# Token halves transposed behind the halves of the projection, and token roots of two orders read back from memory

## The chip, the cores and the metric

The program runs on one core of one Trainium2 chip. The metric is the device time of one execution in microseconds (us). A core has five engines with a queue each: TensorE (PE, with its weight loads as PEld), VectorE (DVE), ScalarE (ACT), GpSimd (POOL) and SyncE (SP), which here only issues transfers.

## The reference

Two groups of tokens, 512 and 1024 of them, go through two layers that share their weights. Each layer is a mixer and then a routed mixture of 16 experts:

```
for layer in range(DEPTH):
    h = rms_norm(x, norm_mix[layer])
    x = x + (mixer_ab if layer % 2 == 0 else mixer_c)(h, ...)
    h = rms_norm(x, norm_ffn[layer])
    x = x + expert_choice_moe(h, w_router[layer], w_gate[layer], w_up[layer], w_down[layer])
```

`rms_norm` multiplies a token by one over the root of its mean square (the token's root) and by a gain. `mixer_ab` projects h once and runs two kinds of attention: A, three patterns of local attention with keys at strides 1, 4 and 16 (a1, a4, a16), and B, dense attention over all keys. `mixer_c` is local attention with a sink. Queries and keys are normed per head and rotated before the scores. All of it is float32.

## The kernel before

The 1536 tokens are 12 tiles of 128. Attention runs in three phases of `attention_phase`: "b" and "a" in the first layer, "c" in the second, each followed or surrounded by output and expert phases that the change leaves alone. In a phase, a list `events` written by class `Work` sets the order of the work, and every engine walks the same list and does its share of each event. The events are:

- ("N", n, half): half of a raw token tile, 512 of its 1024 columns, is brought into hTh and hTl. PE transposes it in four pieces into a room of PSUM (`turn_x`, L971), ACT copies it out as the high part (`x_high_part`, L669), DVE subtracts to get the low part (`x_low_part`, L796). The half came into xb by a transfer that SP issues (`load_x`, L544).
- ("P", p, half): half of the projection of tile p, twelve matmuls (L151 to L153). After the second half ACT empties the result (`evacuate`, L680 and L681) and squares it for the head norms (L688).
- ("T", p): the normed queries and keys of p are transposed by PE (L995, L998), copied by ACT, split by DVE (the last step is kT, L839).
- ("S", u), ("R", u), ("V", g): scores, transposes of the probabilities (L1021) and the product with V (L1037). ("W", q): a quarter of the weights is split by ACT (L658) and DVE (L788).

Tile p is projected while the unit five tiles back is in R and V. In "b" the token tiles are transposed within the first ten projections, in "c" likewise. Phase "a" does six turns of 12 tiles, two for each pattern. Patterns a4 and a16 need the tokens in another order (`order` 1 and 2), so while the second turn of one pattern is projected, the tiles of the next are transposed anew into hTh and hTl. That makes 24 tiles, or 48 halves, in phase "a", beside 24 halves each in "b" and "c".

Every N, T and R takes the next room of psT, and there are two rooms, used in turn. The transpose that takes a room waits until the one two rooms earlier has been copied out (`room_free`). For an N room that is x_low, DVE's subtraction. In phase "a" one tile uses the rooms R (one, or two where the unit has six key blocks), T, N of half 0, N of half 1.

Token roots: after each N, ACT squares the half in place and sums it (`x_square`, L665). POOL turns two sums into the root rt and the term em (`token_root`, four instructions). `load_x` of a later half waits for the squaring (x_squared), because it writes the same buffer; there are 4, 2 and 3 buffers xb in "b", "a" and "c".

Of the kernel before, what the change touches and what calls it, by code (L numbers as in the profile page):

```python
# [7 lines left out]
F32 = mybir.dt.float32  # L8
# [7 lines left out]
P = 128  # L16
SEQ, DEC_SEQ = 512, 1024
TOK = SEQ + DEC_SEQ
NT = TOK // P
# [4 lines left out]
GROUPS = 4  # L24
# [9 lines left out]
WQ = 4  # L34
# [183 lines left out]
class Work:  # L218
# [41 lines left out]
    def projection(self, p, norm):  # L260

        got = []
        for half in range(2):
            if norm is not None and p:
                got.append(("N", norm, half))
            got.append(("P", p, half))
            if self.dense and p and p % NT == 0 and half == 0:
                got += [("W", p // NT * WQ + 2), ("W", p // NT * WQ + 3)]
        if norm is not None and not p:
            got += [("N", norm, 0), ("N", norm, 1)]  # L270
        return got
# [125 lines left out]

def attention_phase(nc, state, name, steps, hT, roots, x_rows, norm_gain, identity, masks, mask0, table, sink=None,
                    ring=None, loaded=None, split=False, follow=None, w_out=None):
# [10 lines left out]
    hTh, hTl = hT  # L410
    rt, em = roots
    NS = len(steps)
# [82 lines left out]
    half_ready, tally = ph.sem("half_ready"), ph.sem("tally")  # L495
    mask_in = ph.sem("mask_in")
    NCONST, NMASK = 1 + NS, (masks is not None) + (sink is not None)
# [17 lines left out]
    def raw_quarter(q):  # L515

        return raw[:, spot_of(q), :, 0:cols(q)]
# [12 lines left out]
    with nc.Block() as block:  # L530

        @block.sync
        def _(sp):
            halves = 2 * len(work.norms)

            def load_x(x):
                if x >= halves:
                    return
                i, t = work.norms[x // 2]
                if x >= XH:  # L540

                    sp.wait_ge(x_squared, x - XH + 1)
                rows = token_rows(x_rows, t, work.kinds[i])
                sp.dma_start(xb[:, x % XH], rows[:, x % 2 * HC:(x % 2 + 1) * HC]).then_inc(x_in[x % XH], 16)  # L544

            def load_w(q):
                if q >= own + WQ * (follow is not None):
                    return
                if q >= RING:

                    i, quarter = divmod(q - RING, WQ)
                    sp.wait_ge(projected, 2 * (i * NT + NT - 1) + quarter // 2 + 1)
                sp.dma_start(raw_quarter(q), weights(q)).then_inc(w_in[(q - have) % RING], 16)

            def load_constants():
# [30 lines left out]
            load_w(4)  # L586
            load_w(5)
            for e in events:
                if e[0] == "N" and 2 * e[1] + e[2] >= early:
# [14 lines left out]
        def _(pool):  # L604
# [36 lines left out]
            for e in events:  # L641
                if e[0] == "N" and e[2] == 1:
                    token_root(e[1])
                if e[0] == "P" and e[2] == 1:
                    if first:
                        pool.wait_ge(const_in, 16 * NCONST)
                        first = False
                    head_roots(e[1])

        @block.scalar  # L650
        def _(act):
# [20 lines left out]
            def evacuate(p):  # L672
                b, (s, _, t) = p % 2, place(p)
                if p >= 2:
                    act.wait_ge(gained, p - 1)
                n = [work.norm_of[i, t] for i in range(p // NT + 1) if (i, t) in work.norm_of]
                if n:
                    act.wait_ge(rt_ready, n[-1] + 1)
                act.wait_ge(projected, 2 * p + 2)
# [59 lines left out]
            for e in events:  # L739
                if e[0] == "N":  # L740
                    x_high_part(e[1], e[2])
                    to_square.append(e[1:])
                    if e[1] == 0 and not dense:
                        squares()
# [1035 lines left out]
def encoder(nc, a, stop=99):  # L1780
# [13 lines left out]
    with ExitStack() as ctx:  # L1794
# [3 lines left out]

        rt = ctx.enter_context(nc.sbuf_tensor("rt", [P, 3, NT], F32))
        em = ctx.enter_context(nc.sbuf_tensor("em", [P, 3, NT], F32))  # L1800
        roots = (rt, em)
        ident = ctx.enter_context(nc.sbuf_tensor("ident", [P, P], F32))
# [23 lines left out]
        with high(0) as wh:  # L1826
            with nc.sbuf_tensor("hTh", [P, KD, TOK], F32R) as hTh, nc.sbuf_tensor("hTl", [P, KD, TOK], F32R) as hTl:
                attention_phase(nc, state, "b",
                                [dict(kind="b", nq=B_NQ, nkv=1, order=0, w=a["w_b"], gain=a["gain_b"], out=by_tile(ob, B_NQ))],
                                (hTh, hTl), roots, x_rows, a["gain_mix"][0], a["identity"], None, 0, a["rope_axial"],  # L1830
                                ring=dict(kept, high=wh, first=0), follow=dict(w=a["w_a"][0][0], cols=6 * HD))
# [3 lines left out]
                                (hTh, hTl), roots, x_rows, a["gain_mix"][0], a["identity"], a["masks"][:, 3 * P:], 3 * P,  # L1835
                                a["rope_a"], ring=dict(kept, high=wh, first=GROUPS * WQ), loaded=arrivals["c_in"], split=True,
                                w_out=out_weights(a["w_out_ab"], "ab_out"))
# [3 lines left out]
        with high(1) as wh:  # L1841
            with nc.sbuf_tensor("hTh1", [P, KD, TOK], F32R) as hTh, nc.sbuf_tensor("hTl1", [P, KD, TOK], F32R) as hTl:
                attention_phase(nc, state, "c",
                                [dict(kind="c", nq=C_NQ, nkv=1, order=0, w=a["w_c"], gain=a["gain_c"], out=by_tile(oc, C_NQ))],
                                (hTh, hTl), roots, y_rows, a["gain_mix"][1], a["identity"], a["masks"][:, 0:3 * P], 0, a["rope_c"],
                                a["sink"], ring=dict(kept, high=wh, first=0), loaded=arrivals["c_in"],
                                w_out=out_weights(a["w_out_c"], "c_out"))
# [52 lines left out]
```

## Time and profile before

| | |
|---|---|
| time, median of 3 runs | 4019.5 us (4018.96 to 4022.48) |
| the profiled execution | 4020.69 us, span 4018.3 us |
| PE busy | 3811.2 us, 95% of the span |
| DVE, ACT, POOL busy | 67%, 53%, 22% |
| mean granted PE clock | 0.975 of full speed |

Times within the trace are in us from the start of the span. Phase "b" ends at 680, "a" runs from 682 to 1190, "c" from 2360 to 2851; the rest is output and expert phases.

### The profile page before, as it was taken

The numbers are of one execution on the slowest core, as the hardware profiler recorded it, in microseconds if no ns is written. First come the engines' busy times: TensorE is split into PE (matmuls) and PEld (weight loads), VectorE is DVE, ScalarE is ACT, GpSimd is POOL, SyncE is SP. The second block draws the span as 40 slices with busy tenths as digits, with TensorE's granted clock in tenths as the row PEclk, the third lists the DMA queues.
The fourth block names the chain that finished last, engine by engine and source line by source line (L and its number), as shares of the span: only waits on it lengthen the run. The fifth ranks groups of instructions, "written<-read, shape, count | busy, mean of one in ns | idle before, by whom it ended". The sixth has DMA issues, their size and how long they took to land. (4 is left out here: it accounts for less than half of the span.)

```text
span 4018.3 us, 75219 instructions
## 1 busy us (share of the span) xinstructions
PE 3811.2 (95%) x27032; PEld 3678.0 (92%) x27032; DVE 2677.1 (67%) x5533; ACT 2138.5 (53%) x3992; POOL 891.0 (22%) x1463
## 2 busy tenths in 40 slices
PE   7999999999979889999999979999896999999998
PEld 7989988999978689999999979999785999999998
DVE  6665664766665677777777747777536777777775
ACT  6554554666642255565556546555323565656554
POOL 5132220444430011111111133332000111211112
PEclk9999999999989889999999989999997999999999
DMA  3000001122124377887788721000335778777874
GB/s 106 11 22 7 25 16 35 46 67 68 52 95 150 128 244 246 250 251 241 245 250 251 242 83 47 32 22 16 136 137 189 238 250 255 244 240 249 255 244 131
DMA packets 489001, 583.91 MB, mean 145 GB/s; under 512 B 18512, under 2 KB 444496, under 8 KB 488784
## 3 DMA queue, kind: packets, MB, share of 16 engines
q1 hardware_dynamic: 470928, 522.40, 39.6%
q0 software_dynamic: 15680, 50.34, 5.8%
q10 hardware_dynamic: 2176, 8.39, 0.5%
q8 instruction: 122, 2.00, 0.2%
q14 instruction: 95, 0.78, 0.1%
HBM read 514.86 MB, written 66.21 MB: 145 GB/s over the span
## 5 line engine op out<-in xcount | busy, mean ns | idle before, releaser
L1654 DVE TENSOR_TENSOR wl<-raw,wh 128x2048 fp32r<-128x2048 f32 x384 | 879.2, 2290 | 284.9 <-ACT wh L1609 271.9
L1609 ACT CAST wh<-raw 128x2048 fp32r<-128x2048 f32 x384 | 733.1, 1909 | 24.2 <-DMA raw<-in_w_gate 21.9
L1753 PE MATMUL ps_g<-xT,wh 128*128 128x384 f32 x2048 | 599.1, 359 | 3.2 <-DVE xT L1660 3.2
L1753 PE MATMUL ps_u<-xT,wh 128*128 128x384 f32 x2048 | 594.8, 357 | 0.0
L1755 PE MATMUL ps_g<-xT,wl 128*128 128x192 f32 x2048 | 478.9, 254 | 0.0
L1755 PE MATMUL ps_u<-xT,wl 128*128 128x192 f32 x2048 | 477.1, 253 | 0.0
L151 PE MATMUL psP<-ring_high,hTh 128*128 128x384 f32 (+1 forms) x1344 | 464.4, 346 | 12.3 <-ACT V L681 5.1
L153 PE MATMUL psP<-ring_high,hTl 128*128 128x384 f32 (+1 forms) x1344 | 445.5, 331 | 0.0
L152 PE MATMUL psP<-ring_low,hTh 128*128 128x384 f32 (+1 forms) x1344 | 445.4, 331 | 0.0
L1037 PEld LDWEIGHTS psO<-V,pT 128*128 128x128 f32 x3456 | 419.8, 192 | 19.1 <-issue 11.7
L1037 PE MATMUL psO<-V,pT 128*128 128x64 f32 x3456 | 416.3, 273 | 3.7 <-ACT pT L725 3.6
L1755 PEld LDWEIGHTS ps_g<-xT,wl 128*128 128x128 f32 x2048 | 388.4, 191 | 0.0
L1755 PEld LDWEIGHTS ps_u<-xT,wl 128*128 128x128 f32 x2048 | 385.8, 190 | 0.0
L1753 PEld LDWEIGHTS ps_g<-xT,wh 128*128 128x128 f32 x2048 | 378.5, 190 | 3.5 <-issue 3.5
L1753 PEld LDWEIGHTS ps_u<-xT,wh 128*128 128x128 f32 x2048 | 376.1, 189 | 0.0
L713 ACT ACTIVATE prob<-psS,nbias 128x384 f32<-128x384 f32 (+4 forms) x480 | 308.1, 648 | 77.3 <-DVE nbias L860 41.1
L725 ACT COPY pT<-psT 128x512 f32<-128x512 f32 (+2 forms) x348 | 182.9, 540 | 242.8 <-PE psT L1021 237.8
L625 POOL TENSOR_TENSOR xg<-xr,gains 128x256 f32<-128x256 f32 (+1 forms) x168 | 130.2, 775 | 785.3 <-ACT V L681 747.5
L151 PEld LDWEIGHTS psP<-ring_high,hTh 128*128 128x128 f32 x1344 | 256.8, 191 | 17.9 <-ACT V L681 7.9
L1556 POOL COPY put_s<-idx 128x1 uint32 x30 | 5.5, 182 | 1185.7 <-DVE cp L1673 1185.7
L1021 PE MATMUL psT<-ident,prob 128*128 128x128 f32 x1728 | 245.1, 276 | 14.5 <-DVE pT L912 4.7
L805 DVE TENSOR_REDUCE ss<-xn 128x4 f32<-128x256 f32 (+1 forms) x168 | 73.6, 438 | 276.3 <-ACT xn L688 276.3
(204 smaller groups left out, 8901.6 us busy)
## 6 DMA issues: line engine op xcount, KB each, us to landing
raw<-in_w_gate SPq DMA_DIRECT2D x128, 1024.0 KB, 5.4
raw<-in_w_up SPq DMA_DIRECT2D x128, 1024.0 KB, 5.2
raw<-in_w_down SPq DMA_DIRECT2D x128, 1024.0 KB, 8.3
xb<-in_x SPq DMA_DIRECT2D x72, 256.0 KB, 2.8
out_y<-yb SPq DMA_DIRECT2D x24, 512.0 KB, 2.6
h_rows<-hb SPq DMA_DIRECT2D x24, 512.0 KB, 3.0
ring_raw<-in_w_a SPq DMA_DIRECT2D x24, 384.0 KB, 4.3
xb<-in_x SPq DMA_DIRECT2D x12, 512.0 KB, 4.9
```

Of the source, the lines that this page charges most:

```text
L151: eng.matmul(out, ah, bh, start=start, stop=False)
L152: eng.matmul(out, ah, bl, start=False, stop=False)
L153: return eng.matmul(out, al, bh, start=False, stop=stop)
L625: pool.tensor_tensor(xg[:, b, :], xr[:, b, :], gains[:, s, :], ALU.mult).then_inc(gained, 1)
L713: ins = act.activation(prob[:, u % 2, c * KC:c * KC + nk * P], psS[:, u % 2, c * 512:c * 512 + nk * P], ACT.Exp, bias=nbias[:, g % 4, x:x ...
L725: act.copy(pT[:, slot, at:at + w], room_of("R", u, k)[:, 0:w]).then_inc(pT_act, 1)
L1021: ins = pe.transpose(room_of("R", u, k)[:, x * P:(x + 1) * P], prob[:, u % 2, c * KC + j * P:c * KC + (j + 1) * P], ident)
L1037: ins = pe.matmul(psO[:, (off + c) * HD:(off + c + 1) * HD], pT[:, slot, at + x * P:at + (x + 1) * P], V[:, k0 + j, kv * HD:(kv + 1) * HD] ...
L1609: act.copy(wh[:, j % SPL], raw[:, j % RAW]).then_inc(w_high, 1)
L1654: dve.tensor_tensor(wl[:, j % SPL], raw[:, j % RAW], wh[:, j % SPL].bitcast(F32), ALU.subtract)\
L1753: both = lambda **fl: pe.matmul(ps[:, f, 0:2 * CAP], wh[:, j % SPL, k, fs], xT[:, k].rearrange("p h c -> p (h c)"), **fl)
L1755: high = lambda: pe.matmul(ps[:, f, 0:CAP], wl[:, j % SPL, k, fs], xT[:, k, 0, :], start=False, stop=False)
```

## The change

Two things are edited. First, `projection` puts each half of the projection ahead of the N of the same number; this concerns all three phases. Second, phase "a" no longer squares its token tiles. The roots of order 0, which phase "b" has computed, are stored to a small tensor in memory, one root and one term for each token, and read back in the orders of a4 and a16 by four transfers with pieces of 8 bytes. `rt` and `em` become the two columns of one tensor `roots`. In phase "a" `load_x` then waits for PE's transpose of the buffer (x_turned) in place of the squaring.

```diff
@@ projection @@
         for half in range(2):
+            got.append(("P", p, half))
             if norm is not None and p:
                 got.append(("N", norm, half))
-            got.append(("P", p, half))
@@ attention_phase @@
-    rt, em = roots
+    rt, em = roots[:, :, :, 0], roots[:, :, :, 1]
+    squaring = name != "a"
@@ load_x @@
                 if x >= XH:
-
-                    sp.wait_ge(x_squared, x - XH + 1)
+                    sp.wait_ge(x_squared if squaring else x_turned, x - XH + 1)
@@ sync @@
+            def reorder_roots():
+                sp.dma_start(roots_out.rearrange("(t p) x -> p t x", p=P), roots[:, 0]).then_inc(roots_stored, 16)
+                sp.wait_ge(roots_stored, 16)
+                for s, st in enumerate(steps[1:], 1):
+                    for first, n in ((0, SEQ), (SEQ, DEC_SEQ)):
+                        stride = STRIDES[st["kind"]][first > 0]
+                        rows = roots_out[first:first + n].rearrange("(u p r) x -> p r u x", p=P, r=stride)
+                        at = roots[:, s, first // P:(first + n) // P].rearrange("p (r u) x -> p r u x", r=stride)
+                        sp.dma_start(at, rows).then_inc(roots_in, 16)
...
             load_w(4)
             load_w(5)
+            if not squaring:
+                reorder_roots()
@@ gpsimd @@
-                if e[0] == "N" and e[2] == 1:
+                if squaring and e[0] == "N" and e[2] == 1:
                     token_root(e[1])
@@ evacuate @@
-                n = [work.norm_of[i, t] for i in range(p // NT + 1) if (i, t) in work.norm_of]
-                if n:
-                    act.wait_ge(rt_ready, n[-1] + 1)
+                if squaring:
+                    act.wait_ge(rt_ready, work.norm_of[0, t] + 1)
+                elif p % (NT * turns) == 0 and s:
+                    act.wait_ge(roots_in, 32 * s)
@@ scalar @@
                     x_high_part(e[1], e[2])
-                    to_square.append(e[1:])
+                    if squaring:
+                        to_square.append(e[1:])
```

Three places show what moves. The first is PE in phase "a", in the second turn of pattern a1, from the end of a projection to the scores of the next tile; the names in brackets are the semaphores waited on, x_low being the low part of an N. Before:

```order
L153 MATMUL psP<-ring_high,hTl 128x384
L1037 MATMUL psO<-V,pT 128x64 [waits pT_act_2,o_done_2]
L1037 MATMUL psO<-V,pT 128x64 x2
L1037 MATMUL psO<-V,pT 128x64 [waits pT_dve_2]
L1037 MATMUL psO<-V,pT 128x64 x2
L1021 MATMUL psT<-ident,prob 128x128 [waits x_low_2,exp_done_2]
L1021 MATMUL psT<-ident,prob 128x128 x2
L1021 MATMUL psT<-ident,prob 128x128 [waits x_low_2]
L1021 MATMUL psT<-ident,prob 128x128 x2
```

The same place with the change (14 lines were added above, so L971 is L985, L1037 is L1051 and L1021 is L1035):

```order
L153 MATMUL psP<-ring_high,hTl 128x384
L985 MATMUL psT<-ident,xb 128x128 [waits low_out_2,x_in1_2]
L985 MATMUL psT<-ident,xb 128x128 x3
L1051 MATMUL psO<-V,pT 128x64 [waits pT_act_2,o_done_2]
L1051 MATMUL psO<-V,pT 128x64 x2
L1051 MATMUL psO<-V,pT 128x64 [waits pT_dve_2]
L1051 MATMUL psO<-V,pT 128x64 x2
L1035 MATMUL psT<-ident,prob 128x128 [waits x_low_2,exp_done_2]
L1035 MATMUL psT<-ident,prob 128x128 x2
L1035 MATMUL psT<-ident,prob 128x128 [waits x_low_2]
L1035 MATMUL psT<-ident,prob 128x128 x2
```

The transposes of the second token half have come from ahead of the twelve matmuls to behind them; the second x_low that the R waits for belongs to that half.

The second place is ACT in phase "a", one tile from the exponentials to the copy of the next probabilities. Before:

```order
L713 ACTIVATE prob,den<-psS,nbias 128x256
L669 CAST hTh<-psT 128x4x128 [waits x_turned_2]
L665 ACTIVATE xb,ssx<-xb 128x512 [waits rt_ready_2]
L669 CAST hTh<-psT 128x4x128 [waits x_turned_2]
L665 ACTIVATE xb,ssx<-xb 128x512 [waits rt_ready_2]
L680 COPY xr<-psP 128x256 [waits projected_2,gained_2]
L681 ACTIVATE V<-psP,rt 128x128
L688 ACTIVATE xn<-xr 128x256 [waits turned_2,evacuated_2]
L725 COPY pT<-psT 128x512 [waits pv_done_2,p_turned_2]
```

The same tile with the change:

```order
L726 ACTIVATE prob,den<-psS,nbias 128x256
L681 CAST hTh<-psT 128x4x128 [waits x_turned_2]
L693 COPY xr<-psP 128x256 [waits projected_2,gained_2]
L694 ACTIVATE V<-psP,roots 128x128
L701 ACTIVATE xn<-xr 128x256 [waits turned_2,evacuated_2]
L681 CAST hTh<-psT 128x4x128 [waits x_turned_2]
L738 COPY pT<-psT 128x512 [waits pv_done_2,p_turned_2]
```

Both squarings are gone, and the cast of the second half now stands behind the three instructions that empty and square the projection.

The third place is SP at the start of phase "a", with the change:

```order
L553 DMA ring_raw<-in_w_a 128x768 x2
L556 DMA roots_out<-roots 128x12x2
L563 DMA roots<-roots_out 128x8
L563 DMA roots<-roots_out 128x8x2
L563 DMA roots<-roots_out 128x8
L563 DMA roots<-roots_out 128x16
L610 DMA arec<-osb 128x132 x6
```

Before, the first output stores (arec) follow directly on the two weight quarters (ring_raw); now the store and the four loads of the roots stand between them.

## Rows read from the trace of the kernel before

**Rows 1.** The page, busy time, its share of the span, instructions.

```profile
PE 3811.2 (95%) x27032; PEld 3678.0 (92%) x27032; DVE 2677.1 (67%) x5533; ACT 2138.5 (53%) x3992; POOL 891.0 (22%) x1463
```

**Rows 2.** Groups by line and shape, 756 to 1040: busy, mean ns | idle before, releasers.

```profile
L971 PE MATMUL psT<-ident,xb 128*128 128x128 f32 x192 | 29.9, 279 | 10.6 <-DVE kT L839 6.0 <-ACT pT L725 3.1 <-DVE pT L912 1.5
```

**Rows 3.** Timeline around a tile of phase "a": start, duration, engine, line, [idle before <-releaser].

```profile
804.07 1.00 PE L1037 MATMUL psO<-V,pT 128*128 128x64 f32 x8
804.32 0.37 ACT L680 COPY xr<-psP 128x256 f32<-128x256 f32 x1 [0.66 <-PE psP L153]
804.90 0.83 PE L1021 MATMUL psT<-ident,prob 128*128 128x128 f32 x6
804.99 0.42 ACT L688 ACTIVATE xn<-xr 128x256 f32<-128x256 f32 x1
...
808.60 0.63 PE L971 MATMUL psT<-ident,xb 128*128 128x128 f32 x4 [1.16 <-DVE pT L912]
...
808.99 0.42 PE L151 MATMUL psP<-ring_high,hTh 128*128 128x384 f32 x1
```

**Rows 4.** Timeline in the fill of phase "b", all engines.

```profile
43.69 0.59 ACT L669 CAST hTh<-psT 128x512 fp32r<-128x512 f32 x1 [0.84 <-PE psT L971]
...
44.31 0.69 DVE L796 TENSOR_TENSOR hTl<-psT,hTh 128x512 fp32r<-128x512 f32 x1 [0.90 <-ACT hTh L669]
...
46.10 0.28 DVE L827 TENSOR_SCALAR xn<-xg,rstd 128x128 f32<-128x128 f32 x1
...
46.44 0.44 PE L995 MATMUL psT<-ident,xn 128*128 128x128 f32 x2 [1.02 <-DVE xn L827]
```

**Rows 5.** Timeline of PE in phase "a", V to R and V to T.

```profile
853.90 1.45 PE L1037 MATMUL psO<-V,pT 128*128 128x64 f32 x12
855.18 0.83 PE L1021 MATMUL psT<-ident,prob 128*128 128x128 f32 x6
...
950.42 1.00 PE L1037 MATMUL psO<-V,pT 128*128 128x64 f32 x8
...
952.18 0.27 PE L995 MATMUL psT<-ident,xn 128*128 128x128 f32 x1
...
979.31 0.55 PE L1037 MATMUL psO<-V,pT 128*128 128x64 f32 x4
...
980.32 0.30 PE L995 MATMUL psT<-ident,xn 128*128 128x128 f32 x1
```

**Rows 6.** PE where a turn ends in phase "a", the timeline.

```profile
862.19 1.08 PE L971 MATMUL psT<-ident,xb 128*128 128x128 f32 x4 [2.56 <-DVE kT L839]
...
1032.14 0.63 PE L971 MATMUL psT<-ident,xb 128*128 128x128 f32 x4 [2.12 <-DVE kT L839]
```

**Rows 7.** Windows: length, PE, PEld, DVE, ACT, POOL busy (x), PEclk, DMA share, GB/s.

```profile
860.00:864.00 4.00, 1.81 (x7) 1.84 (x8) 3.71 (x12) 3.21 (x11) 0.00 (x0) 0.78 0.37 118
...
2404.00:2408.00 4.00, 4.00 (x18) 3.91 (x19) 2.06 (x5) 1.97 (x6) 1.18 (x4) 0.63 0.39 111
```

**Rows 8.** Timeline of PE at the start of phase "c".

```profile
2378.87 0.63 PE L971 MATMUL psT<-ident,xb 128*128 128x128 f32 x4 [1.71 <-DVE hTl L796]
...
2383.37 0.66 PE L971 MATMUL psT<-ident,xb 128*128 128x128 f32 x4 [1.76 <-DMA xb<-out_y]
```

**Rows 9.** Waits of PE, 2350 to 2860: us in total, times, longest.

```profile
PE psT L971 <- DVE kT L839: 4.9, 4, 2.0
```

**Rows 10.** Waits of PE, 0 to 170.

```profile
PE psT L995 <- DVE xn L827: 7.4, 5, 2.3
PE psT L971 <- DVE kT L839: 4.4, 3, 2.9
```

**Rows 11.** Timeline of SP at the start of phase "a".

```profile
688.81 0.80 SPq L553 DMA_DIRECT2D ring_raw<-in_w_a  x2
719.62 19.65 SPq L598 DMA_DIRECT2D arec<-osb  x4
```

**Rows 12.** The page, DMA queues: packets, MB, share of 16 engines.

```profile
q1 hardware_dynamic: 470928, 522.40, 39.6%
```

More of the change, by code:

```diff
@@ L395, in spot, with attention_phase @@
         return u % (self.nq // 2), self.units[u][2][k][0][0] * 3 * P
-def attention_phase(nc, state, name, steps, hT, roots, x_rows, norm_gain, identity, masks, mask0, table, sink=None,
+def attention_phase(nc, state, name, steps, hT, roots, x_rows, norm_gain, identity, masks, mask0, table, roots_out, sink=None,
                     ring=None, loaded=None, split=False, follow=None, w_out=None):
@@ L495, in attention_phase @@
     half_ready, tally = ph.sem("half_ready"), ph.sem("tally")
-    mask_in = ph.sem("mask_in")
+    mask_in, roots_stored, roots_in = ph.sem("mask_in"), ph.sem("roots_stored"), ph.sem("roots_in")
     NCONST, NMASK = 1 + NS, (masks is not None) + (sink is not None)
@@ L1797, in encoder @@
         gate = ctx.enter_context(nc.sbuf_tensor("gate", [P, 64], F32))
-        rt = ctx.enter_context(nc.sbuf_tensor("rt", [P, 3, NT], F32))
-        em = ctx.enter_context(nc.sbuf_tensor("em", [P, 3, NT], F32))
-        roots = (rt, em)
+        roots = ctx.enter_context(nc.sbuf_tensor("roots", [P, 3, NT, 2], F32))
+        roots_out = dram("roots_out", (TOK, 2))
         ident = ctx.enter_context(nc.sbuf_tensor("ident", [P, P], F32))
@@ L1829, in encoder @@
                                 [dict(kind="b", nq=B_NQ, nkv=1, order=0, w=a["w_b"], gain=a["gain_b"], out=by_tile(ob, B_NQ))],
-                                (hTh, hTl), roots, x_rows, a["gain_mix"][0], a["identity"], None, 0, a["rope_axial"],
+                                (hTh, hTl), roots, x_rows, a["gain_mix"][0], a["identity"], None, 0, a["rope_axial"], roots_out,
                                 ring=dict(kept, high=wh, first=0), follow=dict(w=a["w_a"][0][0], cols=6 * HD))
@@ L1835, in encoder @@
                                 (hTh, hTl), roots, x_rows, a["gain_mix"][0], a["identity"], a["masks"][:, 3 * P:], 3 * P,
-                                a["rope_a"], ring=dict(kept, high=wh, first=GROUPS * WQ), loaded=arrivals["c_in"], split=True,
+                                a["rope_a"], roots_out, ring=dict(kept, high=wh, first=GROUPS * WQ), loaded=arrivals["c_in"], split=True,
                                 w_out=out_weights(a["w_out_ab"], "ab_out"))
@@ L1845, in encoder @@
                                 (hTh, hTl), roots, y_rows, a["gain_mix"][1], a["identity"], a["masks"][:, 0:3 * P], 0, a["rope_c"],
-                                a["sink"], ring=dict(kept, high=wh, first=0), loaded=arrivals["c_in"],
+                                roots_out, a["sink"], ring=dict(kept, high=wh, first=0), loaded=arrivals["c_in"],
                                 w_out=out_weights(a["w_out_c"], "c_out"))
```

## The prediction

> **What bounds the kernel now.** I read the page first. PE is busy for 3811.2 us, 95% of the span, and no other engine for more than 67% [rows 1]. So a microsecond counts here only if PE stood idle in it, or comes to stand idle in it. The change touches nothing outside the three attention phases, and in them the question is what PE waits for around the transposes of raw tokens, L971.
>
> The second view groups the instructions of the stretch of phase "a" that holds its 48 token halves. PE stood idle 10.6 us ahead of L971 there: 6.0 us for the low part kT of the queries and keys just transposed, 3.1 and 1.5 us for copies of probabilities [rows 2]. These are waits for a room of PSUM: the transpose comes so soon behind T that the rooms are not yet empty. The reader is to see how small this is, 10.6 us in a stretch of 284. The timeline shows one such wait, 1.16 us at 808.60 [rows 3]. What follows a tile in this stretch is seen there too: PE goes from the projection into V at 804.07 and into R at 804.90, with no gap.
>
> **The order of P and N, gain.** In phase "a" the projection half now stands between T and the first N, and nearly all of the 10.6 us should go. Not all: where a turn ends, the long waits of 2.56 and 2.12 us [rows 6] come from weight splitting that holds ACT and DVE, and the second projection half needs those weights itself, so I keep 1 us of each as idle. With the small gaps under 0.3 us counted back this gives 9.5 us. Behind the first long wait the clock is down: the window that holds it was granted 0.78 of full speed, and the one behind a 2 us wait in phase "c" 0.63, between the two levels of 1.2 and 2.4 GHz [rows 7]. At 0.63, four microseconds do the work of 2.5, so each such place costs some 1.5 us beyond its wait; I take 2 us back for two places in "a" and 1.5 us for the one in "c". Phase "a" gains 11.5 us.
>
> **The order of P and N, loss.** The second half is now transposed behind the projection. The instruction that takes the room after next must wait for DVE's subtraction of it: the second batch of R, or T where R takes one room. Call X the time at which PE is done with the projection, 804.07 [rows 3]. ACT starts the copy of the result 0.25 us after X, and ends the squaring of it at 804.99 + 0.42, which is X + 1.34. Only then comes the cast, since it stands behind these three in ACT's queue. From the start of a cast to the start of the subtraction it is 44.31 less 43.69, 0.62 us, and the subtraction takes 0.69; from the end of a DVE instruction to the PE instruction that waited it is 0.06 us (46.10 + 0.28 to 46.44) [rows 4]. So the room is free at X + 2.7.
>
> PE reaches it sooner. Four transposes hold it for 0.39 us (808.60 to 808.99) [rows 3]. V takes 1.28 us with 12 rows (853.90 to 855.18) and 0.83 us with 8 (804.07 to 804.90), and half an R of six about 0.28 us (0.83 less one transpose, halved) [rows 3, 5]. From V to T it is 1.76 us with 8 rows of V (950.42 to 952.18) and 1.01 us with 4 (979.31 to 980.32) [rows 5]. Of the 24 tiles, by the program's order:
>
> - 6 wait in R after a long V: 2.7 - 0.39 - 1.28 - 0.28 = 0.75 us each, 4.5
> - 2 wait in R after a short V: 2.7 - 0.39 - 0.83 - 0.28 = 1.2 us each, 2.4
> - 8 wait in T: 2.7 - 0.39 - 1.76 = 0.55 us each, 4.4
> - 4 wait in T behind a V of 4 rows: 1.3 us each, less where the scores are longer, 4.9
> - 4 wait in T where V or the scores are longer still: 0.1 to 0.4 us, 1.0
>
> The sum is 17 us, with the four tiles in which a weight quarter follows 18 us. I see nothing that hides it: PE has no gap in this place today. It could be less if ACT's three instructions overlap more than the starts show, down to about 10 us; if x_low came 0.5 us later than I reckon it would be 28 us. Phase "a" is 6.5 us slower by this.
>
> **Phase "c".** The two waits at its start, 1.71 us for a room and 1.76 us for a transfer [rows 8], lie ahead of token halves with a projection ready behind them: 3.5 us gained. The later waits for kT, 4.9 us in four [rows 9], and some 0.7 us of smaller ones go too, and with the clock that is 10.6 us. Against it, "c" still squares. The squaring of the second half moves to the next tile, ahead of the first cast there, and the squaring of the first stays ahead of the copy of the projection, so ACT does this chain later than in "a". V has up to 24 rows here and hides most. Five tiles have R or are next to it; I estimate 0.4 to 2 us for four of them, 5 us. Phase "c" is 5.5 us faster.
>
> **Phase "b".** In its fill, T waits for the normed queries, 7.4 us in five waits [rows 10]. DVE does the rotation and scaling of the tile before behind the second x_low; now they come ahead of it. In steady fill this saves the 0.4 us by which the first half is now later than half a tile less, and at the start, where PE also sits out a late transfer, some 3 us; together 5 us by the time the fourth tile is through. The three waits for kT, 4.4 us [rows 10], become shorter by half, since the low part itself is no earlier: 2.3 us. One R follows directly on a second half with no V between, and waits 2.7 - 0.39 - 0.3, 2 us. Phase "b" is 5 us faster.
>
> **The roots from memory, and no squaring in "a".** ACT loses 48 squarings and POOL 96 small instructions there. Both engines wait for others in that stretch, and the squarings stood ahead of the end of the projection, so they delayed nothing on PE: 0. On SP, a store, a wait for it and four loads stand ahead of the first output store. SP issues its last weight quarter at 689.6 and nothing more until 719.62 [rows 11], so it has 30 us. The trace shows no transfer in 8-byte pieces. From below the price is 0. From above: 4608 pieces, at the mean of all packets of the queue, 39.6% of 16 engines' 4018.3 us over 470928 packets, 54 ns each [rows 12], are 16 us on 16 engines, and only the store's third of it keeps SP. The values are wanted 165 us later. I take 0. It would cost something only from 0.3 us a piece and engine on. The Trainium skill (DMA: Bandwidth & Descriptors, Specifications) asks for at least 512 B a piece for full rate and says that SDMA reads, modifies and writes below it. That speaks against these pieces; it gives no factor, and at twice the mean the sum would be the same.
>
> **Sum.** "a" +6.5, "c" -5.5, "b" -5, roots 0: -4 us against the profiled 4020.7, which is 1.2 us above the median of 4019.5. So 4016.7 for such an execution and 4015.5 at the median; I say 4015.
>
> **The rivals.** What a measurement of this kernel can tell from no change is about 0.2%, 8 us.
>
> - *Gains and new waits cancel* (the forecast, 4012 to 4027): 0.43.
> - *The new waits are mostly covered* (chance 0.35). V and R would not be reached as early as I reckon, or ACT's chain is shorter, say 8 us lost in "a", 1 in "b" and 2 in "c". Then the gains of 11.5, 10.6 and 7.3 us leave -18: 4001. For it: the gains are waits that are in the trace, the losses are only worked out. Against it: every number in X + 2.7 is from a row, and PE has no gap after a projection today.
> - *The second x_low is later than X + 2.7* (0.22), and the kernel slower. The place is ACT: in "b" and "c" it also squares a half ahead of the evacuation, and exponentials stand there. At 0.5 us more in each of the 24 + 9 tiles the loss grows by some 14 us, and the sum turns to +10: 4030. The sign changes at 0.12 us more, and 8 us slower is reached at about 0.4 us. For it: in "c" one squaring more stands ahead of the evacuation than I have priced exactly. Against it: in "a", where 24 of the tiles are, ACT has nothing else between the projection's end and the cast.
> - *The roots' pieces are slow enough to hold SP*: at 0.6 us a piece the store alone would take 58 us and the first output stores come 30 us late, with two output buffers to stop DVE and then PE. That adds 28 us to the sum, 4043. I count 0.02 for it within the slower case. The page of the Trainium skill named above speaks for it; no row here shows pieces that slow.
>
> **How the numbers follow.** Faster by over 0.2% 0.35, within it 0.43, slower 0.22. The range takes in the middle of both neighbours: from 4001, where the new waits are mostly covered, to 4030, where x_low is half a microsecond late. The likeliest case alone is 4012 to 4027.
>
> **What would show it.** In the new trace, in phase "a": the idle time ahead of the token transposes falls from 10.6 to about 2 us; R and T get new waits, named by the low part hTl, of 0.5 to 1.3 us, 20 or so of them, 17 us in sum; the cast of the second half starts 1.3 us after the projection's end. In "c" the waits at the start are gone and the windows behind 2404 are at full clock. In "b" the T of the first tile comes some 3 us earlier. The stores of "a" start when they did, relative to the phase. The prediction is wrong if R does not wait in "a", or if ACT reaches the second cast well before or after X + 1.3.

## The result

| kernel | median (range) | executions |
|---|---|---|
| before, same chip | 4018.96 us (4018.55 to 4022.48) | 5 |
| changed | 3998.3 us (3995.3 to 3999.36) | 5 |

The ratio is 0.9947, 95% interval 0.9934 to 0.996: the change makes the kernel faster by 21 us. The prediction said 4015, with 4001 as its lower end, and is wrong. The profiled execution took 3998.3 us with a span of 3996.5 at a mean clock of 0.977.

The page after, the line that answers to [rows 1]:

```profile
PE 3801.9 (95%) x27032; PEld 3671.0 (92%) x27032; DVE 2677.2 (67%) x5533; ACT 2109.5 (53%) x3896; POOL 857.1 (21%) x1367
```

ACT has 96 instructions less (a squaring is two, one of them reads the sum) and POOL 96. Groups by line and shape after, 750 to 1034, which answers to [rows 2]:

```profile
L985 PE MATMUL psT<-ident,xb 128*128 128x128 f32 x192 | 28.7, 272 | 0.0
```

The 10.6 us are gone entirely. Waits of PE after, 740 to 1060 (us in total, times, longest):

```profile
PE psT L1009 <- DVE hTl L810: 7.0, 12, 1.1
PE psT L1035 <- DVE hTl L810: 3.9, 8, 0.8
```

So the new waits that the prediction described are there, 20 of them, in R and T, on the low part. One of them in the timeline after:

```profile
971.38 0.60 PE L985 MATMUL psT<-ident,xb 128*128 128x128 f32 x4
971.63 0.37 ACT L693 COPY xr<-psP 128x256 f32<-128x256 f32 x1 [1.58 <-PE psP L153]
...
972.31 0.42 ACT L701 ACTIVATE xn<-xr 128x256 f32<-128x256 f32 x1
...
972.63 0.57 ACT L681 CAST hTh<-psT 128x512 fp32r<-128x512 f32 x1
...
973.23 0.69 DVE L810 TENSOR_TENSOR hTl<-psT,hTh 128x512 fp32r<-128x512 f32 x1
...
974.07 0.30 PE L1009 MATMUL psT<-ident,xn 128*128 128x128 f32 x1 [1.08 <-DVE hTl L810]
```

From the end of the projection, X = 971.38, the copy starts at X + 0.25, the cast at X + 1.25 and T at X + 2.69, where the prediction had 0.25, 1.34 and 2.7.

**Where the time came from.** The transposes of queries and keys (T, 168 tiles) are the same work in every kernel here, so their start times can be set against each other tile by tile. A span of start times that is shorter than before is a gain of that stretch:

| stretch | gain | predicted |
|---|---|---|
| phase "b", to its last T | 5.3 us | 5 |
| between the phases, to the first T of "a" | 1.4 | |
| "a", the 24 tiles that transpose tokens (T of tile 59 to T of tile 96) | 3.3 | -6.5 |
| rest of "a", expert phase | 1.9 | |
| "c", its first token transpose to its first T | 5.0 | "c" in all |
| "c", eight tiles more | 6.2 | 5.5 |

That makes 23.0 us; 1.2 are lost again behind it, and the span is 21.8 us shorter. The error of 17.8 us is 9.8 in "a", 5.7 in "c" and 2 us outside. The 1.4 us between the phases go with the clock: the window 682 to 688 before was granted 0.50, the lower of its two levels, and the window 676 to 682 after, which holds about the same work, 0.72. Against the kernel before, the other kernels with the old order in "b" are between 1.2 us later and 1.2 us earlier at its last T, and those with the new order gain 4.4 to 6.7 us, so a difference of 2 us in "b" says nothing. Nor do the 1.4 us between the phases: the kernels below have from -0.5 to +1.4 there, with either order.

### The profile page after: what moved, and what is told of

It is laid out like the page before. It is cut to its first block and busy times, and to the rows that moved or that the text cites. A ratio compares the mean times of both kernels' runs of the same rounds, so it can differ in the third digit from the quotient of the medians.

```text
span 3996.5 us, 74990 instructions
## 1 busy us (share of the span) xinstructions
PE 3801.9 (95%) x27032; PEld 3671.0 (92%) x27032; DVE 2677.2 (67%) x5533; ACT 2109.5 (53%) x3896; POOL 857.1 (21%) x1367
## 5 line engine op out<-in xcount | busy, mean ns | idle before, releaser
L151 PE MATMUL psP<-ring_high,hTh 128*128 128x384 f32 (+1 forms) x1344 | 462.2, 344 | 12.6 <-ACT V L694 5.1
L1051 PEld LDWEIGHTS psO<-V,pT 128*128 128x128 f32 x3456 | 418.9, 193 | 18.7 <-issue 11.7
L1051 PE MATMUL psO<-V,pT 128*128 128x64 f32 x3456 | 417.0, 273 | 3.5 <-ACT pT L738 3.5
L1035 PE MATMUL psT<-ident,prob 128*128 128x128 f32 x1728 | 247.1, 276 | 21.8 <-DVE hTl L810 7.4
L152 PEld LDWEIGHTS psP<-ring_low,hTh 128*128 128x128 f32 x1344 | 255.3, 190 | 0.0
```

What stands on the lines that cost most here:

```text
L151: eng.matmul(out, ah, bh, start=start, stop=False)
L152: eng.matmul(out, ah, bl, start=False, stop=False)
L1035: ins = pe.transpose(room_of("R", u, k)[:, x * P:(x + 1) * P], prob[:, u % 2, c * KC + j * P:c * KC + (j + 1) * P], ident)
L1051: ins = pe.matmul(psO[:, (off + c) * HD:(off + c + 1) * HD], pT[:, slot, at + x * P:at + (x + 1) * P], V[:, k0 + j, kv * HD:(kv + 1) * HD] ...
```

## The experiments

All were timed in five rounds; the kernel before gave 4017.3 to 4019.0 in the three jobs. "Stretch" is T of tile 59 to T of tile 96 in phase "a": 276.96 us before (767.31 to 1044.27), 273.70 after (760.66 to 1034.36). One execution of each kernel was traced. The two kernels with a late release and the one that changes only SP ran on another chip than the others, so where kernels of two jobs are compared, the difference of each to the kernel before of its own job is given too.

### The two parts alone

The first kernel has the new order only, and squares as before:

```diff
+            got.append(("P", p, half))
             if norm is not None and p:
                 got.append(("N", norm, half))
-            got.append(("P", p, half))
```

> The kernel before with the order of P and N alone changed; the roots stay as before and phase a squares. Theory A (the gain comes from the order; the idle time that the trace prints ahead of the token transposes understates what those waits cost): 3999 us, within 3 us of the changed kernel's 3998.3, ratio to before about 0.995. Theory B (taking the squarings off ACT is what made the difference, because they delayed the casts): 4010 us or more, ratio 0.998 or more.

Measured: 4007.02 (4004.2 to 4009.96), ratio 0.9973 (0.9962 to 0.9983). The stretch is 284.08, 7.1 us longer than before.

The second has the changed kernel's roots and release, with the old order in all phases (the diff above reversed).

> The changed kernel with the old order of N and P; the roots are read from memory and phase a does not square. Theory A: within 2 us of before, 4018 us, as the prediction priced the roots at 0. Theory B: 4008 us or less, with the waits for copies ahead of the token transposes in phase a clearly under the 10.6 us of before.

Measured: 4010.88 (4008.95 to 4015.82), ratio 0.9985 (0.9976 to 0.9994). The stretch is 271.25, 5.7 us shorter. So the roots from memory are worth something under either order. That refutes the 0 of the prediction, and both theories in their pure form. Alone the parts bring 0.27% and 0.15%, together 0.53%: one makes the other worth more.

The third keeps the changed kernel, with the old order in phase "a" alone:

```diff
+            ahead = self.kinds[0] in ("a1", "a4", "a16")
+            if norm is not None and p and ahead:
+                got.append(("N", norm, half))
             got.append(("P", p, half))
-            if norm is not None and p:
+            if norm is not None and p and not ahead:
                 got.append(("N", norm, half))
```

> The changed kernel with the old order in phase a alone, the new one in b and c. As the prediction had it (the new order costs 6.5 us in a): 3992 us. Theory A, which reads from the two traces, event against event, that the new order gained 3.8 us over the 24 tiles in a: 4002 us, with the idle time ahead of the token transposes in a back near 10 us and the waits for hTl gone.

Measured: 3995.13 (3993.1 to 3999.21), ratio 0.9943 (0.993 to 0.9957); stretch 271.34. Neither 3992 nor 4002 came out. By the traces the new order in "a" costs 2.4 us once the roots come from memory, and it costs 7.1 without them. What the order gains lies in "b" and "c": between this kernel and the second it is 15.8 us.

### Why the order alone is dear in "a"

Waits of PE in the kernel with the order only, 740 to 1060:

```profile
PE psT L971 <- DMA xb<-in_x: 11.3, 15, 1.3
PE psT L995 <- DVE hTl L796: 3.5, 6, 1.1
PE psT L1021 <- DVE hTl L796: 2.1, 7, 0.4
```

The largest wait is for a token transfer, which neither the kernel before nor the changed one has here. Its timeline:

```profile
793.13 0.66 PE L971 MATMUL psT<-ident,xb 128*128 128x128 f32 x4 [0.68 <-DMA xb<-in_x]
...
798.33 0.63 ACT L665 ACTIVATE xb<-xb 128x512 f32<-128x512 f32 x1
...
799.07 0.33 SPq L544 DMA_DIRECT2D xb<-in_x  x1
...
802.06 0.66 PE L971 MATMUL psT<-ident,xb 128*128 128x128 f32 x4 [1.30 <-DMA xb<-in_x]
```

PE transposes the second half of a tile at 793.13. ACT squares it only at 798.33, since it comes up behind the projection and the squaring stands at the next P event, behind the copy of the probabilities and two exponentials. Only then is the transfer of the next tile's second half issued, at 799.07, and it takes 3 us to land; PE has waited 1.30 us for it at 802.06. In the kernel before, the two squarings of a tile start 2.9 and 1.4 us behind their transposes (here it is 5.2 us), and the half issued at 802.59 is wanted at 808.60. In the changed kernel the transpose at 798.15 lets SP go on, and the next second half is wanted at 806.82. So a new theory: what the roots bring is the release of the transfer, not the time of ACT or POOL.

To test it, the roots stay in memory, and the squarings and POOL's instructions are put back as work without a reader (two squarings of 192 elements instead of one of 512, since no larger room was free):

```diff
+                for k, done in enumerate((spare_done, x_squared)):
+                    if x + k:
+                        act.wait_ge(x_squared if k == 0 else spare_done, x + k)
+                    act.activation(spare[:, :].rearrange("p (k c) -> p k c", k=2), spread(ident[:, 0:96], 1, 2),
+                                   ACT.Square, accum_out=ssx[:, n % 2, h:h + 1]).then_inc(done, 1)
...
-                if squaring and e[0] == "N" and e[2] == 1:
+                if e[0] == "N" and e[2] == 1:
                     token_root(e[1])
```

> The changed kernel, with ACT's and POOL's root work of phase a put back as work whose result nobody reads: two squarings of 192 elements per token half (at least the time of the one that was removed) and POOL's four instructions, while the token transfer is still released by PE's transpose. Theory A (the roots from memory pay through the release of the token transfer, and so through SP's queue; ACT's and POOL's time is worth nothing): as the changed kernel, 3998, within 3 us; no waits for xb in phase a, the two waits at the turn ends stay gone. Rival (ACT's time between the projection and the cast pays): as the new order alone with squaring, about 4007.

Measured: 3998.9 (3994.97 to 4000.47), ratio 0.9947 (0.9933 to 0.996), the same as the changed kernel; stretch 274.18. Its page:

```profile
PE 3801.9 (95%) x27032; PEld 3670.1 (92%) x27032; DVE 2677.8 (67%) x5533; ACT 2146.4 (54%) x4088; POOL 891.9 (22%) x1463
```

And its waits of PE, 740 to 1060:

```profile
PE psT L1019 <- DVE hTl L820: 6.6, 11, 1.1
PE psT L1045 <- DVE hTl L820: 4.2, 9, 0.8
```

ACT is 37 us busier and POOL 35, and with the new order it costs nothing. Then the same kernel with its one wait set back:

```diff
-                    sp.wait_ge(x_squared if squaring else x_turned, x - XH + 1)
+                    sp.wait_ge(x_squared, x - XH + 1)
```

> The kernel with the new order, the roots from memory and the dummy squarings (3998.9), with one wait changed: the token transfer of phase a waits for the dummy squaring again and not for PE's transpose. Theory A (the release is what pays): back to the time of the new order alone, 4007 (4005 to 4010), with waits for xb of about 11 us in phase a. Rival (something else in the roots' path pays): 3999.

Measured: 4010.49 (4007.65 to 4012.95), ratio 0.9982 (0.9973 to 0.9991); stretch 286.73. Waits of PE, 740 to 1060:

```profile
PE psT L995 <- DMA xb<-in_x: 14.3, 15, 1.5
PE psT L1019 <- DVE hTl L820: 3.1, 5, 1.1
PE psT L1045 <- DVE hTl L820: 2.2, 7, 0.4
```

The waits for xb are back, and the time is 3.5 us above the 4007 of the theory's forecast, just outside its range. With this order the release alone is worth 11.6 us of the time (13.1 when each kernel is taken from the kernel before of its own job) and 12.6 us of the stretch: it takes away 14.3 us of waits for transfers and uncovers 5.5 us of waits for the low part.

### The old order, and the end of a turn

The same two kernels with the old order, first with the early release:

> The same with the old order of events in all phases: roots from memory, dummy squarings and POOL's work kept, release by the transpose. Theory A: as the roots with the old order, 4011, within 3 us, weight quarters at the turn ends issued two us earlier. Rival (ACT's time pays): as before, 4017 to 4019.

Measured: 4016.31 (4013.11 to 4018.73), ratio 0.9992 (0.9983 to 1.0001); stretch 275.18, with a low clock at one place that takes 1.8 us of it. Theory A, 4011 within 3 us, failed; the time is next to the rival's 4017. So with the old order ACT's and POOL's time is not worth nothing. Put back, it costs 5.4 us against the second kernel (3.8 when each is taken from its own job) and 3.9 us of the stretch: the low clock's 1.8, 0.7 at the two turn ends, and 1.4 in small waits elsewhere. What was put back is somewhat more than what was removed, 37 us of ACT for 29.

Second with the late release:

> The same two edits with the old order of events: dummy squarings, and the token transfer released by them. Theory A: as before, 4018 to 4020, and the long waits at the turn ends back at 2.6 and 2.1 us. Against the same kernel with the early release (4016.3, or 4014.5 with a low clock in phase a that its trace shows at one place counted back) this gives what the release alone is worth in the old order, 3 to 4 us. Rival: the same time as with the early release, 4016.

Measured: 4016.87 (4012.75 to 4021.95), ratio 1.0003 (0.9994 to 1.0012); stretch 275.86, with the same low clock. The release alone is worth 0.7 us in the old order by the traces (0.6 by the medians, 2.0 when each is taken from its own job), not 3 to 4: my expectation failed. So did the one on the waits at the turn ends. They are, in this kernel's timeline:

```profile
861.79 0.63 PE L995 MATMUL psT<-ident,xb 128*128 128x128 f32 x4 [1.70 <-DVE kT L863]
...
1030.75 0.63 PE L995 MATMUL psT<-ident,xb 128*128 128x128 f32 x4 [2.71 <-DVE kT L863]
```

With the early release they are 1.70 and 2.04. Only the second came back. In the old order the next half is wanted some 6 us after its transfer is issued, and nobody waits for it. The gain of 5.7 us in the second kernel must have another source, and the end of a turn shows most of it. The kernel before, a timeline of SP and ACT ahead of the long wait of [rows 6]:

```profile
852.44 0.33 SPq L544 DMA_DIRECT2D xb<-in_x  x1
853.12 1.32 SPq L553 DMA_DIRECT2D ring_raw<-in_w_a  x2
...
854.96 0.91 SPq L553 DMA_DIRECT2D ring_raw<-in_w_a  x2
...
857.62 2.13 ACT L658 ACTIVATE ring_high<-ring_raw,gn 128x384 fp32r<-128x384 f32 x4 [1.43 <-DMA ring_raw<-in_w_a]
```

SP takes its instructions in order. The token half at 852.44 waits for a squaring, the weight quarters stand behind it, and the split at 857.62 has waited 1.43 us for them. The changed kernel:

```profile
845.62 0.80 SPq L553 DMA_DIRECT2D ring_raw<-in_w_a  x2
...
848.16 0.80 SPq L553 DMA_DIRECT2D ring_raw<-in_w_a  x2
...
850.60 2.14 ACT L670 ACTIVATE ring_high<-ring_raw,gn 128x384 fp32r<-128x384 f32 x4
```

Less the 5.5 us by which this kernel is ahead at the T before, the split starts 1.5 us earlier. One kernel tests this by itself: the kernel before, and on SP alone, where a turn ends in "a", the quarters are issued ahead of the token half.

```diff
-                if e[0] == "N" and 2 * e[1] + e[2] >= early:
-                    load_x(2 * e[1] + e[2] + XH)
+                if e[0] == "N" and 2 * e[1] + e[2] >= early:
+                    late_x.append(2 * e[1] + e[2] + XH)
...
+                if name != "a" or not (e[0] == "N" and following[0] == "P" and following[1] % NT == NT - 1):
+                    if e[0] != "P":
+                        for x in late_x:
+                            load_x(x)
...
                     for quarter in (0, 1):
                         load_w(e[1] // NT * WQ + RING + 2 * e[2] + quarter)
+                if e[0] == "P":
+                    for x in late_x:
+                        load_x(x)
```

> The kernel before with one change on SP: where a turn ends in phase a, the two weight quarters are issued ahead of the token half that waits for a squaring. Theory A (the wait at the turn end is a late weight quarter behind a blocked SP): quarters issued up to 2 us earlier, the waits of 2.56 and 2.12 us at most half as long, 4 to 5 us in all with the clock: 4014. Rival (the split itself holds ACT and DVE, whenever the quarter comes): 4018, waits unchanged.

Measured: 4016.35 (4012.78 to 4018.43), ratio 0.9995 (0.9986 to 1.0004). The time can't be told from no change, and the medians don't confirm 4014. In its trace the stretch is 272.49, 4.5 us shorter, 2.36 and 2.09 of it between the tiles at the two turn ends, and nothing elsewhere in it. The second kernel had 2.34 and 2.07 in the same places. Against that its phase "b", which the edit doesn't touch, is 1.2 us later. The waits of PE at the two turn ends, in this kernel's timeline:

```profile
862.69 0.63 PE L982 MATMUL psT<-ident,xb 128*128 128x128 f32 x4 [1.45 <-DVE kT L850]
...
1030.50 0.63 PE L982 MATMUL psT<-ident,xb 128*128 128x128 f32 x4 [0.98 <-DVE kT L850]
```

They were 2.56 and 2.12 [rows 6]. So the late quarter accounts for 1.1 us of each wait. The rest of what the two places gain goes with the clock. Two windows before, behind the two waits:

```profile
864.00:868.00 4.00, 4.00 (x26) 4.00 (x26) 0.89 (x2) 1.57 (x5) 1.67 (x5) 0.80 0.34 110
1034.00:1038.00 4.00, 4.00 (x24) 4.00 (x23) 0.65 (x3) 1.34 (x5) 1.75 (x5) 0.71 0.01 2
```

Behind the shorter waits the clock stays full, and it does so too in the kernel with the old order and the late release, behind 1.70 and 2.71 us. So this share is not tied to the quarter alone, and each kernel has only one trace.

Of the 5.7 us of the roots in the old order, 4.4 lie at the two turn ends, as much as the order on SP brings there by itself. Another 0.6 is one wait of T in the trace before, 0.54 us for DVE's last scaling (L827) at 919.40. It is there in the three kernels that compute the roots in "a", and in none that reads them from memory, with or without the work put back. Why isn't known, nor what makes up the last 0.7 us, a few tenths at a time.

### The position of the second half

> The changed kernel; in phase a the cast of the second token half stands ahead of the squaring of the projection on ACT (and the subtraction ahead of the sum on DVE). If the room's release is the chain that the prediction wrote down (projection done, evacuation, squaring, cast, subtraction), it comes 0.4 us earlier, at 2.25 us instead of 2.7 us behind the projection's end, and each of some 21 tiles that wait gains up to that: 3990 us. If something else ends those waits (DVE's own queue, PE), nothing changes: 3998 us.

In phase "a" of the changed kernel, ACT's cast of the second half stands ahead of the squaring of the projection, and DVE subtracts ahead of its sum:

```diff
                         evacuate(e[1])
-                        square(e[1])
+                        if late_square(at):
+                            unsquared = e[1]
+                        else:
+                            square(e[1])
...
                     x_high_part(e[1], e[2])
+                    if unsquared is not None:
+                        square(unsquared)
+                        unsquared = None
```

Measured: 3987.67 (3983.58 to 3990.16), ratio 0.9924 (0.991 to 0.9937), faster than the kernel before and the changed one; stretch 263.93, 9.8 us shorter than in the changed kernel, for 24 tiles with a 0.42 us instruction less in the chain (10.1). The timeline at the place shown above:

```profile
964.17 0.60 PE L996 MATMUL psT<-ident,xb 128*128 128x128 f32 x4
...
964.95 0.59 ACT L684 CAST hTh<-psT 128x512 fp32r<-128x512 f32 x1
...
965.57 0.69 DVE L819 TENSOR_TENSOR hTl<-psT,hTh 128x512 fp32r<-128x512 f32 x1 [2.00 <-ACT hTh L684]
...
966.41 0.30 PE L1020 MATMUL psT<-ident,xn 128*128 128x128 f32 x1 [0.63 <-DVE hTl L819]
```

The chain is X + 2.24 instead of X + 2.69 and the wait 0.63 instead of 1.08. Nothing in "a" stands against it. The same move in "c" as well:

> The kernel with the cast ahead of the squaring of the projection in phase a (3987.7), and the same move in phase c. Phase c lost 1.9 us to hTl in the changed kernel, so by the chain 3986, and the waits for hTl in c gone. Rival: in c the squaring of the projection then comes later and T waits for it: 3990 or more.

Measured: 3988.9 (3983.56 to 3992.15), ratio 0.9923 (0.9909 to 0.9936): no difference from the one in "a" alone. The waits for the low part in R of "c" fell from 1.9 to 1.4 us and not to none, so the 2 us expected aren't there.

At last the order P0, N0, N1, P1:

```diff
             got.append(("P", p, half))
-            if norm is not None and p:
-                got.append(("N", norm, half))
+            if norm is not None and p and half == 0:
+                got += [("N", norm, 0), ("N", norm, 1)]
```

> The changed kernel with the events of a tile in the order P0, N0, N1, P1: both token halves between the halves of the projection. The second half has twelve matmuls behind it again, so R and T of phase a should not wait for hTl: the 15 us lost there in the changed kernel are not lost. But the second N comes only a transpose's length behind the first, 2.9 us behind T as before, so the waits for kT come back, some 6 to 8 us. By that 3991 (3987 to 3996). Rival (the second N waits for pT and kT as much as R saves): 3998.

Measured: 4011.87 (4007.66 to 4014.23), ratio 0.9982 (0.9973 to 0.9991), 20 us above what I expected. In "a" it does much of what it should, stretch 268.91, 4.8 us shorter than in the changed kernel. But I had worked it out for "a" alone, and in the other phases it takes the gains of the order back: "b" -0.8 us where the changed kernel has +5.3, from the first token transpose of "c" to its ninth T +1.9 in place of +11.2. Waits of PE, 0 to 170, in this kernel:

```profile
PE psT L1009 <- DVE xn L841: 7.1, 5, 2.3
PE psT L985 <- DVE kT L853: 5.2, 2, 3.4
```

And in the changed kernel:

```profile
PE psT L1009 <- DVE xn L841: 5.2, 6, 1.9
...
PE psT L985 <- DVE kT L853: 1.1, 1, 1.1
```

With a token half ahead of the second projection half, DVE's subtraction of it again stands ahead of the rotation and scaling for T, and these are the waits of [rows 10]. So what "b" and "c" gain comes from the second half standing behind the whole projection, which is also what makes R and T wait in "a".

## Why the prediction was wrong

**Phase "b": right.** 5 us predicted, 5.3 measured, and 4.4 to 6.7 in all kernels with the new order there. The parts were less exact: the one R directly behind a second half waits 1.5 us (2 predicted), the waits for the normed queries fell only from 7.4 to 5.2, and those for kT from 4.4 to 1.1, more than by half.

**The roots: a step that failed.** The prediction gave "the squarings stood ahead of the end of the projection, so they delayed nothing on PE: 0" and looked at ACT, at POOL and at the queue for the new pieces. Measured, the roots are worth 8.7 us on top of the new order (4007.0 to 3998.3) and 6.4 us alone (4017.3 to 4010.9). ACT's and POOL's time is worth nothing with the new order (37 and 35 us of it put back, 3998.9 against 3998.3), but not with the old one. But the release of `load_x`, which was on record as part of the change, was priced nowhere. In the new order a transfer released by the squaring is late: 11.6 us, shown by the pair that differ in one wait. In the old order the release holds SP ahead of the weight quarters: the trace of the kernel that changes only SP gains 4.4 us at two turn ends, clock included, though the times don't confirm it. The two don't add up in the changed kernel: of the 7.2 us that it gains at the turn ends from T to T, the order alone has 6.4, with the late release.

This step explains why the parts came out as they did, but hardly the error of the sum. The prediction's account of the order in "a" takes every transfer to be in time, and with the early release, which is in the changed kernel, it is. The 11 us of waits that it didn't see and the 11 us that take them away cancel there. What made the sum wrong are the terms of the order, in "a" and in "c".

**The order in "a": the steps that the sum failed by.** The chain was right to 0.1 us: X + 2.69 for X + 2.7, 20 waits in the places named. Its two sums were not. Split each of the 24 tiles at X, the end of the projection, and count the four moved transposes as 0.43 us (765.64 to 766.07 after). From T to X the changed kernel is then 17.4 us shorter, where the prediction had a gain of 11.5, and from X to the next T it is 14.6 us longer, where it had a loss of 18. With the 0.6 us of the wait at 919.40 that comes to the 3.3 us of the table within 0.1. Of the 14.6 us 10.9 are printed as waits.

Of the gain, 8.2 us lie at the two turn ends, where 4.7 were counted. The gain was held down there by "I keep 1 us of each as idle". They went entirely, with the low clock behind them. The reason that I gave for keeping them, splitting that holds ACT and DVE, may be what is left in the old order with the quarters on time (1.45 and 0.98 us), which no run tests. In the new order nothing is left, and this is so with the late release too: the order alone gains 3.8 us from T to T at the first turn end, as the changed kernel does (3.7), and 2.6 at the second (3.4).

The other 9.2 us, for which 6.8 were counted, are small waits that cost more than they print, since the profile counts idle time from the modelled end of a matmul: from T at 806.93 to the transposes at 808.60 [rows 3] it is 1.67 us where tiles without a wait have 0.39 (775.35 to 775.74 before), 1.28 for a wait shown as 1.16. Tiles with no printed wait gain up to 0.2 us as well.

That the order alone measured -7.1 beside the -6.5 of the prediction is a coincidence. It contains 11.3 us of waits for transfers of which the prediction knew nothing, and less of the waits that it named.

**Phase "c": right in kind, the gain too small and the loss too large.** The loss of 5 us was an estimate without rows. Waits of PE after, 2330 to 2850:

```profile
PE psP L151 <- DVE ring_low L802: 3.2, 4, 0.8
PE psT L1035 <- DVE hTl L810: 1.9, 2, 1.1
```

Before, the first of these was 2.4 us in three waits and the second wasn't there, so the printed price is 2.7 us. With 11.2 us left over, the gain was 13.9 us and not 10.6. Some 11 us of it are printed waits that are gone, the 4.9 for kT of [rows 9] among them; the rest goes with the clock, which was low at 2404 [rows 7] and is full there after.

**The store and the loads of the roots: right, with a wrong count.** SP after, at the start of "a":

```profile
685.44 0.43 SPq L556 DMA_DIRECT2D roots_out<-roots  x1
692.78 2.26 SPq L563 DMA_DIRECT2D roots<-roots_out  x4
712.97 5.95 SPq L610 DMA_DIRECT2D arec<-osb  x2
```

The store is complete 7.3 us after its issue, and the first output store is issued 18 us after the last of the loads, at 712.97. It comes 6.65 us earlier than the 719.62 of [rows 11], just as much as T of the first tile is earlier. The DMA view after, 685 to 700:

```profile
DMA packets 3385, 0.96 MB, mean 64 GB/s; under 512 B 3071, under 2 KB 3071, under 8 KB 3383
```

Of the 3071 small packets 127 have 4 bytes and are not of the roots. The other 2944 are the 1536 pieces of 8 bytes of the store and 1408 of the loads: 1024 of 8 bytes, 256 of 32 and 128 of 64. Only one of the four loads has pieces of 8 bytes, and the prediction's 4608 pieces should have been 2944. The store's packets all run between 688.21 and 689.33 and take 9 ns each, against 54 ns for the mean packet [rows 12] and the 0.3 us from which it would have cost something. The Trainium skill (DMA: Bandwidth & Descriptors, Specifications) asks for at least 512 B a piece for full rate and says that smaller pieces are read, modified and written. The trace agrees as to the rate: 8 bytes in 9 ns is far below the 1.1 KB in 54 ns of the mean packet. It cost nothing here, since nobody waited; whether anything is read and modified doesn't show.

**The rivals.** "The new waits are mostly covered" had the right time (4001) for the wrong reason, which is luck: the waits weren't covered (14.6 us of them in "a", for 8 in that rival), other gains were missing from the sum. The rival in which the second low part comes late has nothing for it.

## What to carry to other kernels

When a change alters which event releases a transfer, follow that release through the issuing queue before pricing the instructions that were removed: here the weight quarters behind the blocked issue were late too. Work that is free under one order can cost under another: test it in both. A wait put down to an engine that splits or copies is worth a look at that engine's own input; here both turn-end waits named DVE, and 1.1 us of each came from a weight quarter that SP issued late. And an order that is worked out for one phase has to be summed over all phases that share its code.

## What the runs showed of the hardware

- A squaring with a sum is two instructions on ACT: 0.65 us for 512 elements, and 0.21 us for the read of the accumulator.
- 1536 pieces of 8 bytes from SBUF to memory took 9 ns each on their DMA engines and ran within 1.1 us; the store was complete 7.3 us after its issue.
- Nearly equal waits can cost the clock or not. Behind the wait of 2.12 us at 1032.14 the clock fell to 0.71 in the window, and behind one of 2.71 us at the same place of the kernel with the old order and the late release it stayed at 1.00. In the kernel with the old order, the squarings kept and the early release, a 1.29 us wait at 806.65 came before a low clock. Its window 808 to 812:

```profile
808.00:812.00 4.00, 4.00 (x18) 3.90 (x18) 2.44 (x9) 2.90 (x11) 0.00 (x0) 0.63 0.25 70
```

Before, with 1.16 us at the same place [rows 3]:

```profile
808.00:812.00 4.00, 3.40 (x23) 3.39 (x24) 3.84 (x15) 2.39 (x9) 0.88 (x1) 1.00 0.06 17
```

The granted clock of the first lies between its two levels of 1.2 and 2.4 GHz. That decided 1.8 us, far more than the difference of the waits.
